# Row sums of four norms by one wide matmul, and five smaller edits, in a two-block transformer kernel on one core

## What is computed

```python
def rms_norm(x, g):                       # rms_norm_2 is the same
    y = x * lax.rsqrt(jnp.mean(x * x, axis=-1, keepdims=True) + EPS)
    return y * g

# first block
h = rms_norm(x, mix_norm);       z = h @ w_in            # "mix"
x = x + concat([gla(z), swa(z)]) @ w_out                 # "wout"
h2 = rms_norm(x, ffn_norm)                               # "ffn"
u = causal_dwconv(h2 @ w_up, conv_w, conv_b)             # "upA", "upB"
x = x + (silu(a) * b) @ w_down                           # "downA", "downB"
# second block, layer 0
m = conformer_conv(rms_norm(h, mix_pre_g[0]), ...)       # "pre0": pw1, conv, layer norm, pw2
h = h + rms_norm(m, mix_post_g[0])                       # "post0"
f = squared_relu_mlp(rms_norm(h, ffn_pre_g[0]), ...)     # "ffpre0": ff1, ff2
h = h + rms_norm(f, ffn_post_g[0])                       # "ffpost0"
# layer 1
k_nope, k_rope, v = mla_shared_kv(h, ...)                # "kvpre", dkv
m = mla_attention(rms_norm(h, mix_pre_g[1]), ...)        # "pre1": dq ... wo
h = h + rms_norm(m, mix_post_g[1])                       # "post1"
f = squared_relu_mlp(rms_norm(h, ffn_pre_g[1]), ...)     # "ffpre1"
h = h + rms_norm(f, ffn_post_g[1])
```

## Time and profile before

| | us |
|---|---|
| median of 3 runs | 1718.32 |
| lowest, highest | 1717.58, 1721.27 |
| the profiled execution, its own time | 1716.32 |
| its span in the trace | 1714.5 |
| TensorE busy | 1699.4 (99%) |
| VectorE busy | 938.5 (55%) |
| ScalarE busy | 605.7 (35%) |
| GpSimd busy | 187.5 (11%) |

### The profile page before, as it was taken

The page is one execution under the profiler, slowest core; times in us unless marked ns, Lnnn a source line. Parts: engine busy times, 40 slices in busy tenths (PEclk is TensorE's granted clock), DMA queues, the critical chain, the costliest instruction groups (busy, mean ns, idle before and its releaser), DMA issues.

```text
span 1714.5 us, 21902 instructions
## 1 busy us (share of the span) xinstructions
PE 1699.4 (99%) x8100; PEld 1363.0 (79%) x8100; DVE 938.5 (55%) x1251; ACT 605.7 (35%) x892; POOL 187.5 (11%) x159
## 2 busy tenths in 40 slices
PE   9999999999999999999999999999999999999998
PEld 7878888888888866587888888878788788888886
DVE  5775546753666399757532343365874653234432
ACT  4564434432444332344321222243453432122221
POOL 0210201100111101111200111100001021001111
PEclk9999999999999999999999999999999999999999
DMA  6211222232323255221332232212202133223221
GB/s 234 74 50 53 96 83 93 92 133 87 97 89 96 85 168 151 83 86 50 112 104 92 97 97 90 95 62 86 74 13 87 62 101 103 92 97 97 93 80 49
DMA packets 48884, 157.92 MB, mean 92 GB/s; under 512 B 7088, under 2 KB 7728, under 8 KB 48816
## 3 DMA queue, kind: packets, MB, share of 16 engines
q1 hardware_dynamic: 48288, 155.52, 28.4%
q10 hardware_dynamic: 528, 1.46, 0.3%
HBM read 146.14 MB, written 2.10 MB: 86 GB/s over the span
## 4 chain that ended last, share of the span: by engine, by line
PE 95%; DVE 3%; ACT 1%; issue 1%; SPq 1%; DMA 0%; DVEq 0%; ACTq 0%
PE bank L1143 27%; PE bank L1144 26%; PE bank L1145 26%; PE bank L1691 2%; PE bank L1294 1%; PE bank L1300 1%; PE bank L1295 1%; PE bank L1858 1%; PE bank L1187 1%; PE bank L1233 1%; SPq L491 1%; PE bank L1876 1%; DVE w_lo L1964 0%; PE bank L1181 0%; PE bank L1221 0%
## 5 line engine op out<-in xcount | busy, mean ns | idle before, releaser
L1964 DVE TENSOR_TENSOR w_lo<-w_raw,w_hi 128x1024 fp32r<-128x1024 f32 x269 | 346.9, 1292 | 306.2 <-ACT w_hi L687 183.5
L1143 PE MATMUL bank<-a_hi,w_hi 128*128 128x512 f32 x1156 | 457.5, 396 | 0.1
L1144 PE MATMUL bank<-a_lo,w_hi 128*128 128x512 f32 x1156 | 452.9, 392 | 0.0
L1145 PE MATMUL bank<-a_hi,w_lo 128*128 128x512 f32 x1156 | 452.3, 391 | 0.0
L1144 PE MATMUL bank<-g_lo,w_hi 128*128 128x512 f32 x688 | 269.5, 392 | 0.0
L1145 PE MATMUL bank<-g_hi,w_lo 128*128 128x512 f32 x688 | 269.2, 391 | 0.0
L1143 PE MATMUL bank<-g_hi,w_hi 128*128 128x512 f32 x688 | 269.0, 391 | 0.0
L1143 PEld LDWEIGHTS bank<-a_hi,w_hi 128*128 128x128 f32 x1156 | 217.1, 188 | 54.5 <-issue 6.1
L1145 PEld LDWEIGHTS bank<-a_hi,w_lo 128*128 128x128 f32 x1156 | 217.1, 188 | 47.6
L1144 PEld LDWEIGHTS bank<-a_lo,w_hi 128*128 128x128 f32 x1156 | 217.3, 188 | 46.4 <-issue 1.0
L687 ACT ACTIVATE w_hi<-w_raw 128x1024 fp32r<-128x1024 f32 x153 | 159.6, 1050 | 157.8 <-PE bank L1145 144.7
(11 more groups left out here) (289 smaller groups left out, 1798.0 us busy)
## 6 DMA issues: line engine op xcount, KB each, us to landing
w_raw<-in_stream SPq DMA_DIRECT2D x269, 512.0 KB, 3.5
shifted<-u_pad SPq DMA_DIRECT2D x120, 66.5 KB, 2.0
h<-in_xT SPq DMA_DIRECT2D x8, 256.0 KB, 5.9
out<-h SPq DMA_DIRECT2D x8, 256.0 KB, 2.1
cst_b<-in_consts SPq DMA_DIRECT2D x1, 896.0 KB, 9.7
cst_b<-in_consts ACTq DMA_DIRECT2D x1, 896.0 KB, 4.5
shifted<-u_pad ACTq DMA_DIRECT2D x8, 66.5 KB, 2.1
tap_cols<-in_vectors SPq DMA_DIRECT2D x16, 29.8 KB, 1.8
```

Of the source, the lines that this page charges most:

```text
L1143: pe.matmul(out, w0, x0, start=start, stop=False, skip_group_check=loose)
L1144: pe.matmul(out, w0, x1, start=False, stop=False, skip_group_check=loose)
L1145: return pe.matmul(out, w1, x0, start=False, stop=stop, skip_group_check=loose)
L1964: dve.tensor_tensor(w_lo[slot][:, :], w_raw[slot][:, :], f(w_hi[slot][:, :]), ALU.subtract)\
```

## The change

Six edits, all in the code of norms and of the start.

1. Wide sums for "ffn", "pre0", "ffpre0", "ffpre1". One matmul of 512 columns, with a 128x128 block of ones as the stationary operand and the summed squares as the moving one, gives each token's sum on all 128 partitions at once, in bank 4. ACT takes the root of it into `r_pre` (128x512), DVE the reciprocal in place (128x512). The two sums of `stat`, the 128x4 root and reciprocal, the four `spread` matmuls and the copy are gone for these norms. POOL adds one tile more (upA, pw1), DVE folds once more (ff1a). The sum stands after the sixth operand tile of upA and pw1 (before: after the eighth), and where it stood in ff1a. "mix" folds once more too and keeps the narrow form on one tile.
2. Banks. The first three tiles of ff1a and pw1 go to banks 5 to 7. In upA the fifth to seventh tile do. The second group of four tiles of upA and ff1a is written out ahead of the loop, and its first three tiles wait for no read.
3. The first weight unit is loaded, rounded and split in halves of 128x512; its first half is issued ahead of the first `h` tile. Three warm-up matmuls are left of four.
4. After pw2 and wo ACT squares each tile from its bank (for pw2 with the bias inside the square), and DVE's copy waits for that square.
5. For "pre1" DVE adds the squares of tiles 2i and 2i+1, and PE sums four tiles instead of eight.
6. A sigmoid of one column follows the root of "pre0" on ACT.

```diff
+WIDE = ("ffn", "pre0", "ffpre0", "ffpre1")
...
+        def own_bank(name, i, j):
+
+            first = {"upA": 1, "ff1a": 0}.get(name)
+            return bank[j + 5 if first is not None and isinstance(i, int) and i == first and j < 3 else j]
...
+            sp.dma_start(w_raw[0][:, 0:SEQ], stream[u0 * P:(u0 + 1) * P, 0:SEQ]).then_inc(first_landed, 16)
             sp.dma_start(h[:, 0:SEQ], xT[0:P, :]).then_inc(h_landed[0], 16)
-            load(0, 0)
+            sp.dma_start(w_raw[0][:, SEQ:], stream[u0 * P:(u0 + 1) * P, SEQ:]).then_inc(w_landed[0], 16)
...
-                for k in range(1, STAT_TILES[name] - 1):
+                for k in range(1, STAT_TILES[name] - (name not in WIDE)):
...
+            def wide_root(name):
+
+                act.wait_ge(stat_done, STAT_NO[name] + 1)
+                act.activation(r_pre[:, :], bank[4][:, :], ACT.Sqrt, bias=small[:, 60:61]).then_inc(rms_ready, 1)
...
-            take_root("pre0", r_pre)
+            wide_root("pre0")
+            act.activation(small[:, 63:64], small[:, 60:61], ACT.Sigmoid)
...
-                    act.wait_ge(out_read, TILE0[product] + k + 1)
                     if k == 7:
                         load_sqrt(STAT_NO[stat])
-                    square(stat, k, T(m, k))
+                    if per_tile_units == 1:
+                        act.wait_ge(unit_used, UNIT0[product] + k + 1)
+                        square(stat, k, bank[k % 4][:, :], bias=b_pw2_d[:, k:k + 1] if product == "pw2" else 0.0)
...
+            def pair_sum(k):
+
+                pe.wait_ge(sq_pairs, k // 2 + 1)
                 for b in range(NB):
                     last = pe.matmul(bank[5][:, b:b + 1], T(T(m, k), b, P), cst[:, ONES:ONES + 1],
...
+                if name in WIDE:
+                    last = pe.matmul(bank[4][:, :], cst[:, ONES:ONES + P], T(m, 0), start=True, stop=True)
...
+            def wide_stat(name):
+
+                pe.wait_ge(sum_added, ADD0[name] + STAT_TILES[name] - 1)
+                pe.wait_ge(r_ready, R_NO[STATS[STAT_NO[name] - 1][0]] + 1)
+                pe.matmul(bank[4][:, :], cst[:, ONES:ONES + P], ssum[:, :], start=True, stop=True)\
+                    .then_inc(stat_done, 1)
...
+                    if k == 5:
+                        wide_stat(split)
...
-                        if sums:
-                            tile_sum(sums, k - 1)
+                        if sums and k % 2 == 0:
+                            pair_sum(k - 2)
...
-            for _ in range(4):
+            for _ in range(3):
                 pe.matmul(bank[7][:, :], ssum[:, 0:P], ssum[:, :], start=True, stop=True)
...
+                    for j in range(4):
+
+                        unit_ready(n0 + 4 + j)
+                        if j == 3:
+                            pe.wait_ge(out_read, TILE0[name] + 4)
+                        free = bank[j if split in IN_M or j == 3 else 5 + j]
+                        tile_of_eight(n0 + j, (n0 + j) % RING, free[:, :], a_hi, a_lo)
...
+            def wide_r(name):
+                dve.wait_ge(rms_ready, STAT_NO[name] + 1)
+                dve.reciprocal(r_pre[:, :], r_pre[:, :]).then_inc(r_ready, 1)
...
-                for w in (4 * SEQ, 2 * SEQ):
+                for w in (4 * SEQ, 2 * SEQ, SEQ):
...
-                unit_done(n)
+                dve.wait_ge(sq_ready, SQ0["post0"] + k + 1)
...
+            def add_pair(k):
+
+                dve.wait_ge(sq_ready, SQ0["pre1"] + k + 2)
+                dve.tensor_tensor(T(m, k), T(m, k), T(m, k + 1), ALU.add).then_inc(sq_pairs, 1)
```

139 lines of the change are left out of this document (83 added, 56 removed).

## The result

The changed kernel takes 1700.0 us (median of four, 1698.9 to 1701.8) where the kernel before takes 1719.2 (1717.6 to 1721.3): a ratio of 0.989, with an interval of 0.987 to 0.991. The forecast was 1703.9, in a range of 1701.0 to 1708.0. It is faster, as forecast, but by more than the range allowed. The profiled execution took 1698.9, 17.4 less than the profiled one of before, where 14.4 was forecast. The median lies 1.1 above it, where 2.0 was taken over from the kernel before. These two differences, 3.0 and 0.9, are the miss.

The account below looks back on a forecast made before the run. TensorE's queue was taken to bound the kernel, 95% of the last chain. Gains of 5.25 + 0.8 + 3.6 + 2.9 + 1.5 + 0.4 = 14.45 gave 1701.9 profiled and a median of 1703.9, range 1701.0 to 1708.0.

Parts of the forecast that it names:

- only three of these places have a wait: TensorE waits only at the start, at the first taps behind pw1, and at the sum behind pw2 and wo.
- rival 4: Layer norm's clock fall is spared, 1701.7, or the same loss hits another norm, 1706.1; chance 0.12, half on each side.
- Wide sums, 1.75 each: In ffn, ffpre0 and ffpre1, narrow sums and spread cost 2.71, the wide sum 0.96: gain 1.75 each, 5.25 together.
- mix 0.8 and dkv 3.6: Mix loses eight of sixteen narrow passes, gain 0.80; dkv loses four of eight tile sums, gain 3.6.
- The reciprocal: On VectorE at 128x512, 3.0 us by the line through 4 and 16 columns; hidden, so cost 0.
- Rival 1: The 128x512 reciprocal takes 4.4 us, taps gain 1.5, ff1a's weights come late: loss 2.2, 1706.1; chance 0.12.
- pw1 and the taps, 2.9: Behind pw1 `r_pre` comes 2.9 earlier and so do the taps: 1.75 of work and 1.15 of wait.
- The start, 1.5: Weight halves land at 4.1 and 5.5, `h` at 4.8; first product at 6.35 instead of 7.86: gain 1.5.
- Rival 3: At the start the halves don't land apart, or something else takes the gain back: 1705.4; chance 0.08.
- Squares, 0.4: Behind pw2 and wo squares come 0.8 sooner, but TensorE's own queue ends the wait: gain 0.2 each, 0.4 in all.
- Banks, 0: Free banks in upA and ff1a let TensorE's next tiles wait for no read; no gain was counted for them.
- Rivals 2 and 5: Dkv's adds hold TensorE up, 1705.9, chance 0.08; shorter warm-up leaves TensorE at 1.2 GHz, 1723.9 with 40 us, chance 0.02.

Follow-up runs that it names:

- the banks alone: Changed kernel with all undone but the free banks, the third fold and the sigmoid's early table: 1714.0 us, ratio 0.997 to the kernel before.
- the additions: Kernel before plus two idle matmuls in the seventh head's 2.6 us wait and 128 columns of ones in layer norm sums: 1717.9 us.
- the old banks: Changed kernel with first tiles of upA and ff1a in banks 0 to 2 again, later tiles waiting for reads: 1708.0 us, taken again 1708.4.

## Why the prediction was wrong

The mechanism held: TensorE's queue was the limit, and each piece taken off it paid. What failed are sizes, and two terms that stood at nothing. Of the 3.0 that the profiled pair gained beyond the sum, 1.4 is the clock in the layer norm, 0.6 is a wait for a bank in both ff1a, against the sentence "only three of these places have a wait", 0.55 is the term of the taps, 0.5 the sums, 0.2 the squares, 0.15 the rest, and the start gave back 0.4. The 0.9 between profile and median come last. The range's lower edge stood only 0.7 under rival 4's lower case, not the margin of one that was named (at the upper edge it was 1.9); with one full us the measured 1700.0 would still have been outside.

**The sum was 14.45, the work 15.6 to 16.** Step by step:

- *Wide sums, 1.75 each.* 1.8 each. The narrow form was costed right, 2.7; the wide sum was costed as 0.96, a matmul and a change of form. The rows give 0.86 with the change in it. In both ff1a a term was missing, 0.3 each: the fifth tile waited for the bank of the first, which was read only once `r_pre` of the earlier trace rows was there. In the trace of before it shows as a product 0.43 behind the one ahead of it instead of 0.23, and the next one is late by 0.1 as well:

```profile
801.27 0.40 PE L1145 MATMUL bank<-a_hi,w_lo 128*128 128x512 f32 x1
801.70 0.50 PE L1143 MATMUL bank<-a_hi,w_hi 128*128 128x512 f32 x1
802.04 0.39 PE L1144 MATMUL bank<-a_lo,w_hi 128*128 128x512 f32 x1
```

- *mix 0.8 and dkv 3.6.* 0.9 and 3.7. The eight narrow passes and the four sums are the best hit, by the same rows.
- *The reciprocal.* 3.35, not 3.0: the line through 4 and 16 columns was 10% short at 512. The estimate from the Trainium skill's repeat count of 8 (VectorE: DVE Perf Modes, "Walkthrough: the 8-slice pipeline in each mode") was 4.4; the trace, at 6.2 ns for each further column, agrees with neither, but is nearer to the line. Rival 1 is out. It cost nothing, as claimed: the room was 0.65 at the tightest place.
- *pw1 and the taps, 2.9.* 3.45. The sum stood 12.4 after the stage's start, as forecast, and the reciprocal was done 0.45 late, 0.35 of it by its own length. The step that failed is "from `r_pre` to the copies' landing nothing changes, 17.4": it was 16.5, since SP issues the sixteen copies in 10.4 instead of 11.4. All profiles with the change have 10.4 to 10.6, the one with the banks alone too; the two of the kernel before, without and with the additions, have 11.4 and 11.5. So it comes neither from `r_pre` nor from the wide sum. The traces show what stands there. In both of these two one of the copies is followed by the next only after 2.01 and 1.71, where no other profile has over 1.02, and in that pause 16 KB move on a queue for instructions. Of the kernel before, 605.3 to 607.0:

```profile
q8 instruction: 1, 0.02, 5.3%
```

  In the other 15 profiles no such transfer falls among the sixteen copies; in the changed kernel the next one comes at 612.2, 6 behind them. That SP pauses for its own code is a guess from this; what is shown is that the two coincide. Which of the edits moved it wasn't tried.
- *The start, 1.5.* 1.1 in the profile, 0.8 in the middle one of eleven. The step that failed: landed "at 4.1, `h` at 4.8". The first half was taken up at 4.3 to 4.6 in the eleven, and `h` at 5.1 to 6.0; in the profile it is 4.45 and 5.10, so there the halves were 0.65 apart but both 0.3 late. TensorE's three warm-up matmuls also took until 6.8 in that profile, not 6.0: its granted clock rose at 6.6, where it rose at 5.0 in the profile before, and a pass at the lower level took 0.85 instead of 0.43. Rival 3 was half true.
- *Squares, 0.4.* 0.6 by the stages, 0.4 by undoing them. The reason, TensorE's own queue, holds.
- *Banks, 0.* The text gave them the work of keeping TensorE from waiting, but no price. The waits that they spare, 4.4 beside wide sums, are no gain over the kernel before, save the 0.3 in each ff1a. Its median, though, had some 2.5 to gain: banks alone bring 4.6, of which 2.1 are work by the fastest spans at equal clock, 1711.7 and 1713.8 (mix, the lighter sums of ff1a, the bank waits).

**The clock, rival 4.** It was there, on its gaining side: 1.4 from profile to profile, as the clock fell later in the layer norm and was down for 3.4 instead of 6.8. Worked out for it was 2.2. It is no property of the change: three profiles of the same changed kernel show falls in the layer norm in all three (8.6, 8.3 and 9.8 long, 10.0 before), behind the wait for probabilities in two, and at 160 in one. The Trainium skill's rule (TensorE: Matmul & The Clock Gate, "Part 1: The HAM clock gate"), a monitor that runs free of the kernel, agrees with that scatter. What failed is giving one side 0.06 and adding nothing else to it: with the terms of work a little short, that case ended below the range.

**From profile to median.** The prediction lowered the median by the same 14.4 as the profile, that is, it took the 2.0 between the two for a constant. They are no constant. Over all groups the median of the kernel before is 1718.5. Without its 22 scattered executions it is 1717.5, and those of the rest with the mean clock of the profile, 0.998, have 1715.9. So about half of the 2.0 is the scatter, which the free banks take away, and the other half is the clock: the profiled execution had fewer falls than most, as 52 of the 73 have a mean clock of 0.997 or less. The changed kernel has no scatter, and a median clock of 0.998 beside its profile's 0.999. No row of one profile could show this; that the runs of before went from 1717.6 to 1721.3 could have been a hint.

**Rivals 2 and 5** are out: no wait in dkv, and behind the shorter warm-up the first products run at the higher clock. The exception is the first profile with the old banks: TensorE waited 2.1 there, and the clock, which had risen in the warm-up, fell again at 7.6, for 1.5 us of loss.

## What to carry to other kernels

Price a wait by what it does to TensorE behind it as well as by its length: here one of 2.2 to 6 for an operand or a bank cost, where the clock fell behind it, another 0.7 to 2.5, and behind one TensorE went on at a 1.9% longer pitch for a whole loop. A free bank that costs nothing is worth having even where the profile at hand shows a wait of a third of a microsecond. And compare the spread of two kernels' executions, not only their profiles: the lowest ones at the same mean clock give the difference in work, and what the median has beyond it needs a cause of its own. Undo a part together with what was moved for its sake: the sigmoid's table, left at its new place, made the narrow sums look worse than they were.

## What the runs showed of the hardware

- TensorE has two pitches for fp32r products of 512 columns at a granted clock of 1.00, 0.2289 and 0.2333, and keeps one over hundreds of products. Why it takes one or the other stays open: in one profile it changed at 244 with no wait that the trace shows. A stretch over a whole loop stands in two of the four profiles with waits for banks and in none of the 13 with free banks, which do have it for up to 13 us ahead of a sum. The counts of slow executions, 22 of 73 against none of 67, say the same; by what means the free banks do it is not shown.
- The clock fell to 0.50 behind a single wait of 2.2 to 2.6 in some executions and not in others of the same kernel, and behind each of four waits of 3.6 to 6.1. Behind the wait of 2.6 it fell in 9 of 14 profiles, and in none of three with two idle matmuls in the wait.
- In the layer norm it fell in all 13 profiles with token sums of one column, and in none of four with 128 columns.
- In both profiles in which a 16 KB transfer on the queue for instructions fell among SP's sixteen copies, one copy came 1.0 to 1.1 late; in the 15 others none did.
- A reciprocal on 128x512 takes 3.35 on VectorE, five times another operation of that shape.
